# A three-layer attention stack on one core: order of projections, copies and loads around the starts of passes, and one semaphore count

## The chip, the cores and the metric

One core of a Trainium2 chip. The metric is the device time of one execution in microseconds (us), lower being better, given as the median of the runs shown. Engines: PE (TensorE), DVE (VectorE), ACT (ScalarE), POOL (GpSimd), SP (SyncE). A core is written by hand: each engine has its own list of instructions in program order, and semaphores tie the lists together.

## What is computed

One sequence of 1024 tokens of width 1024 goes through three layers, all in float32. Cut to what matters here:

```python
# layer 1: three mixers on the same projection
o_gla = gla_mixer(...)        # gated linear attention, 4 heads
o_dsa = dsa_mixer(...)        # top-256 keys by an indexer, then attention, 6 heads
y_pool = pool_mixer(...)      # windowed means
x = x + concat(y_gla, y_dsa, y_pool) @ w_out
# layer 2: "forgetting" attention, 16 heads, and a gated per-layer input
logit[t, s] = q_t . k_s / sqrt(d) + c[t] - c[s],  c = cumsum(log_sigmoid(h @ w_f + b_f))
h = h + (softmax(logit) @ v * silu(z)) @ w_out;  h = h + (p @ w_up) * sigmoid(h @ w_gate)
# layer 3: dilated attention, 8 heads, each the softmax over three patterns
DIL_PATTERN = ((128, 1), (512, 4), (2048, 16))       # window, stride
o = sum(softmax(stack(lses))[g] * attention_g(q_g, k_g, v_g))
h = h + (o * silu(z)) @ w_out;  h = h + (p @ w_up) * sigmoid(h @ w_gate)
```

## The kernel before

Activations lie transposed, features on the partitions and tokens in two halves of 512. A float32 product is made of three products of rounded parts: `products` (lines 887 to 889) multiplies high by high, high by low and low by high. One projection tile, `half_T`, is 8 such triples into one bank of PSUM, `proj[half]`; ACT copies it out (`projected`, line 1782). Counters join the two: PE waits on `pass_free[half]` before it fills the bank, ACT on `pass_done[half]` before it copies. A tile named X (`half_X`, line 916) turns the transposed values of a head around with 4 transposes through the same bank. Weights stream by SP into two slots and POOL splits them into high and low parts (lines 760 and 762).

The attention layers run in passes: 3 pairs of heads (`dsa`), 8 pairs (`fox`), 8 heads (`dil`). A pass has 8 steps of 128 query rows. While PE works through the steps of pass p, it also makes the projections of pass p+1, a few half tiles per step; `ORDER` names the tiles of a pass (for `dil` thirteen, `TTTTTTTTXTXTX`, so 26 halves), and `proj_units(kind, t)` gives the halves of step t in two parts. In the last pass no projections are left (`follow` is False).

A step of `dil` is this chain: PE makes the scores of a step in two pieces, each in its own bank (lines 1327 and 1336); DVE adds the distance bias piece by piece (line 2380, three adds a step) and takes the maximum (line 2390); ACT takes the exponential (line 1852); PE transposes the result (line 1357); ACT copies that (line 1862); PE multiplies with the values (lines 1380 and 1385); DVE scales (line 2403); PE turns the output (line 1346); DVE gates it (line 2424). `dil_sread` counts the second and the third add of each step, one for each piece. Before PE overwrites the scores of step s, piece b, it waits for `2s + b` of them:

```python
wait_pass(pe, S["sread"], p, N * pieces, s * pieces + piece)
```

On PE a pass of `dil` begins with the scores of steps 0 and 1, which wait until all 13 tiles are copied; on ACT it begins with the exponential of step 0, the store of the row of the head before (line 1788), and the tanh of the gate (line 1873).

The sparse attention (`dsa`) is started while DVE still sorts for the indexer: MAX8 and MATCH_REPLACE8 rounds (lines 2236 and 2238), between which DVE does other work at fixed rounds, among it `pool_outputs(1)`, which reads PE's `pool_products(1)` (line 1120). PE then makes the bias tables (line 1017) and the first scores (line 1182). ACT issues the loads of the bias rows (`load_bias`, line 1704) and the stores from its own queue. In its last pass PE also turns the reloaded input x tile by tile (`residual_turn`, line 1229), which SP loads (line 719) between the loads of finished rows (`finished_rows`, `late_row`, lines 675 and 681); `late_row` waits for the store of pass 1.

In the forgetting attention the rows of c go to memory (line 2020) and come back spread over the partitions (`decay`, line 1758), both issued by ACT.

## Time and profile before

| | us |
|---|---|
| runs, device time | 2986.93, 2995.12, 2994.61 (median 2994.61) |
| profiled execution, device time | 2991.6 |
| its span, first to last instruction | 2989.5 |
| PE matmul busy | 2841.3 (95%) |
| DVE, ACT, POOL busy | 1141.5, 900.4, 1022.8 |

The mean granted clock of TensorE in the profiled execution is 0.972 of full speed. Indexer and linear attention fill the first 480 us, the sparse attention runs to about 650 us, the forgetting attention from about 770 to 1410 us, the dilated attention from 1635 to 2790 us. A row of the timeline gives the start, the duration, the engine, the line and operation, `output<-input` by the program's names, the shape and the count of merged instructions; in brackets stands how long the engine was idle before and what released it. The profile counts some matmuls that the program writes once as two (32 in the profile for 16).

### The profile page before, as it was taken

The page shows a single profiled execution, that of the slowest core. Times are in us where ns is not written, and L with a number is a line of the kernel's source. Part 1 is how long each engine was busy: PE and PEld are TensorE (multiplying, and loading weights), DVE is VectorE, ACT ScalarE, POOL GpSimd, SP SyncE. Part 2 cuts the span into 40 slices and gives each one's busy share as a digit, 9 for nine tenths or more (in the row PEclk, how much of TensorE's full clock was granted, in tenths as well). Part 3 has the DMA queues.
Part 4 walks back from the last instruction along what each step waited for, and adds up shares of the span by engine and source line. Part 5 has one row for each costly group of instructions (what it writes and reads, how often), then busy time and mean ns, then how long its engine had stood idle before and what let it go on. Part 6 is the DMA issues. An engine that isn't in the chain of part 4 may idle for free.

```text
span 2989.5 us, 39787 instructions
## 1 busy us (share of the span) xinstructions
PE 2841.3 (95%) x16428; PEld 2208.0 (74%) x16428; DVE 1141.5 (38%) x2501; ACT 900.4 (30%) x1693; POOL 1022.8 (34%) x443
## 2 busy tenths in 40 slices
PE   6989998999899999999999999999999999998998
PEld 4756676667677777776887877778787878786886
DVE  7998995556422222224334011111111111114323
ACT  4322313552333333334113122222222222223112
POOL 2533392133222222223632433333333323333541
PEclk8989999999999999999999999999999999999998
DMA  4100121121211111112122111111111111113211
GB/s 100 41 22 22 29 67 58 57 78 37 65 39 35 48 50 50 50 43 92 57 78 64 43 43 36 43 42 44 43 43 36 43 43 43 42 44 127 71 44 62
DMA packets 222367, 155.02 MB, mean 52 GB/s; under 512 B 26294, under 2 KB 209116, under 8 KB 222060
## 3 DMA queue, kind: packets, MB, share of 16 engines
q1 hardware_dynamic: 210220, 122.62, 14.3%
q10 hardware_dynamic: 11968, 29.87, 2.7%
q8 instruction: 130, 2.13, 0.3%
q14 instruction: 49, 0.40, 0.0%
HBM read 132.99 MB, written 19.47 MB: 51 GB/s over the span
## 4 chain that ended last, share of the span: by engine, by line
PE 84%; DVE 7%; ACT 3%; issue 3%; POOL 2%; DMA 1%; ACTq 0%; DVEq 0%; SPq 0%; POOLq 0%
PE proj L887 21%; PE proj L889 20%; PE proj L888 20%; PE score L1182 3%; PE score L1197 3%; PE out L1212 3%; DVE arena L2236 1%; PE score L1327 1%; DVE arena L2238 1%; PE out L1380 1%; PE out L1385 1%; PE score L1357 1%; POOL w_lo L762 1%; POOL w_hi L760 1%; PE score L1336 1%
## 5 line engine op out<-in xcount | busy, mean ns | idle before, releaser
L887 PE MATMUL proj<-act_hi,w_hi 128*128 128x512 f32 x2560 | 1033.6, 404 | 21.4 <-ACT hT L1782 8.4
L888 PE MATMUL proj<-act_lo,w_hi 128*128 128x512 f32 x2560 | 1005.7, 393 | 0.0
L889 PE MATMUL proj<-act_hi,w_lo 128*128 128x512 f32 x2560 | 1005.5, 393 | 0.0
L760 POOL TENSOR_TENSOR w_hi<-w_raw,ones 128x1024 fp32r<-128x1024 f32 x177 | 425.4, 2404 | 1695.1 <-PE proj L889 1676.4
L887 PEld LDWEIGHTS proj<-act_hi,w_hi 128*128 128x128 f32 x2560 | 486.9, 190 | 135.0 <-issue 26.3
L889 PEld LDWEIGHTS proj<-act_hi,w_lo 128*128 128x128 f32 x2560 | 485.7, 190 | 105.0
L888 PEld LDWEIGHTS proj<-act_lo,w_hi 128*128 128x128 f32 x2560 | 487.2, 190 | 96.6 <-issue 0.2
L762 POOL TENSOR_TENSOR w_lo<-w_raw,w_hi 128x1024 fp32r<-128x1024 f32 x181 | 446.4, 2466 | 97.5 <-ACT w_hi L1936 83.6
L1782 ACT ACTIVATE arena<-proj 128x512 f32<-128x512 f32 x236 | 175.2, 752 | 691.5 <-PE proj L889 663.4
L2380 DVE SCALAR_TENSOR_TENSOR arena<-arena,score 128x256 f32<-128x256 f32 (+1 forms) x192 | 76.9, 428 | 770.9 <-PE score L1327 724.1
L2276 DVE CUSTOM_DVE_ANT_0 arena<-arena,score 128x512 f32<-128x512 f32 (+2 forms) x192 | 102.7, 572 | 371.1 <-PE score L1182 364.5
L1808 ACT ACTIVATE arena<-score 128x512 f32<-128x512 f32 (+3 forms) x264 | 116.0, 489 | 217.5 <-PE score L1197 217.3
L2236 DVE MAX8 arena<-arena 128x8 f32<-128x640 f32 (+5 forms) x176 | 162.6, 924 | 5.3
L2238 DVE MATCH_REPLACE8 arena<-arena 128x640 f32<-128x640 f32 (+5 forms) x176 | 159.8, 908 | 0.0
L1798 ACT ACTIVATE arena<-arena 128x256 f32<-128x256 f32 (+7 forms) x176 | 135.1, 773 | 68.5 <-DVE arena L2276 41.5
L1197 PEld LDWEIGHTS score<-ident,arena 128*128 128x128 f32 x792 | 87.1, 142 | 79.2 <-issue 48.8
L1782 ACT ACTIVATE hT<-proj 128x512 f32<-128x512 f32 x78 | 65.7, 849 | 260.7 <-PE proj L889 245.3
L1197 PE MATMUL score<-ident,arena 128*128 128x128 f32 x792 | 119.8, 285 | 7.2 <-ACT arena L1798 6.7
L1182 PE MATMUL score<-arena 64*128 64x512 f32 (+3 forms) x432 | 101.5, 547 | 0.7 <-DVE arena L2288 0.7
L887 PE MATMUL proj<-res_parts,w_hi 128*128 128x512 f32 x256 | 101.5, 397 | 0.0
L889 PE MATMUL proj<-res_parts,w_lo 128*128 128x512 f32 x256 | 101.4, 396 | 0.0
L888 PE MATMUL proj<-res_parts,w_hi 128*128 128x512 f32 x256 | 101.4, 396 | 0.0
(260 smaller groups left out, 2881.3 us busy)
## 6 DMA issues: line engine op xcount, KB each, us to landing
w_raw<-dil_w_in_dram SPq DMA_DIRECT2D x80, 512.0 KB, 3.7
w_raw<-fox_w_in_dram SPq DMA_DIRECT2D x32, 512.0 KB, 4.1
w_raw<-w_in_dram SPq DMA_DIRECT2D x23, 512.0 KB, 3.8
y_scratch<-arena ACTq DMA_DIRECT2D x21, 512.0 KB, 4.7
act_lo<-y_scratch SPq DMA_DIRECT2D x21, 512.0 KB, 6.0
arena<-decay_scratch ACTq DMA_DIRECT2D x16, 512.0 KB, 6.8
w_raw<-ple_w_gate_dram SPq DMA_DIRECT2D x16, 512.0 KB, 3.9
arena<-x_dram SPq DMA_DIRECT2D x12, 512.0 KB, 4.0
```

The source lines that it names most:

```text
L760: pool.tensor_tensor(hi, raw, one.unsqueeze(1).broadcast_to([P, KB, P]), ALU.mult).then_inc(w_hi_done, 1)
L762: pool.tensor_tensor(lo, raw, hi.bitcast(F32), ALU.subtract).then_inc(w_split, 1)
L887: pe.matmul(bank, hi, a_hi, start=first, stop=False)
L888: pe.matmul(bank, hi, a_lo, start=False, stop=False)
L889: return pe.matmul(bank, lo, a_hi, start=False, stop=last)
L1182: mm = pe.matmul(score[:, 0, hh * 512:hh * 512 + w], Q["q"][0][rows, i * P:(i + 1) * P], Q["k"][0][rows, lo:lo + w], start=not masked, sto ...
L1197: mm = pe.transpose(score[:, 1, hh * 512 + b * P:hh * 512 + (b + 1) * P], R["p"][hh][i % 2][:, (b0 + b) * P:(b0 + b + 1) * P], ident[:, :])
L1782: act.activation(dst, src, ACT.Copy, scale=scale if role == "q" else 1.0).then_inc(pass_free[half], 1)
L1798: act.activation(R["p"][hh][i % 2][:, 0:width], R["p"][hh][i % 2][:, 0:width], ACT.Exp, bias=R["st"][:, s:s + 1], scale=-1.0, accum_out=R[ ...
L1808: act.activation(R["pT"][hh][:, q % 2, 0:nb * P], score[:, 1, hh * 512:hh * 512 + nb * P], ACT.Copy).then_inc(S["te"], 1)
L2236: dve.max(top8, scores[:, 0:w]).then_inc(IX["top"], 1)
L2238: dve.match_replace(row, top8, row, -3e38).then_inc(IX["top"], 1)
```

## The change

It has five parts.

1. Dilated scores wait for `2(s-1) + b + 1` adds: those of the same piece in the step before.
2. `proj_units` leaves out the last tile of a pass (X, both halves), holds at most two halves in the first part, and puts the second half of an X tile and what follows it into a third part, the tail. For `dil` that changes steps 5 and 6: step 5 was X8.0, X8.1, T9.0, scores of step 7, values; it is X8.0, scores, X8.1, T9.0, values. Step 6 was T9.1, X10.0, X10.1, values; it is T9.1, X10.0, values, X10.1 (the number is the place in `ORDER`, the digit behind the point the half). The last tile X12 is made at the start of the pass that uses it: half 0 behind the scores of step 0, half 1 behind those of step 1. PE waits for one tile fewer at the start, and for the last one before the values of step 0. ACT copies X12 behind the exponential and the store, ahead of the tanh.
3. At the start of the sparse attention two of the four half tiles of pass 2 made ahead (`PAIR_HALVES[2:4]`) move behind `pool_products(1)` and the bias tables, one behind each of the first two score steps; ACT copies them behind the first exponential. `load_bias` is issued one copy sooner.
4. `late_row("dsa")` moves on SP from ahead of the reload of x tile 2 to ahead of that of tile 4.
5. `decay(0, 0)` of the forgetting attention moves on ACT behind two copies of projections.

```diff
@@ proj_units @@
-    units = [(h // 2, h % 2, None) for h in range(first, last)]
-    early = 2 if kind == "dil" else 1
-    return units[:early], units[early:]
+    units = [(h // 2, h % 2, None) for h in range(first, last) if h // 2 < len(ORDER[kind]) - 1]
+    ready = [u for u in units if ORDER[kind][u[0]] != "X" or u[1] == 0]
+    n = next((i for i, u in enumerate(units) if u not in ready), len(units))
+    early = min(n, 2)
+    return units[:early], units[early:n], units[n:]
@@ SP @@
-                    sp.wait_ge(pass_done[half], base + PASSES[kind] * len(ORDER[kind]))
+                    sp.wait_ge(pass_done[half], base + PASSES[kind] * len(ORDER[kind]) - (1 if kind == "dil" else 0))
                         finished_rows("dsa", C_DSA)
+                    if t == 4:
                         late_row("dsa")
@@ PE, sparse attention @@
                     scores(0, 0)
+                    if kind == "dsa" and p == 0:
+                        project(2, [(b, half, None) for b, half in PAIR_HALVES[2:3]])
                     scores(1, 0)
+                    if kind == "dsa" and p == 0:
+                        project(2, [(b, half, None) for b, half in PAIR_HALVES[3:4]])
...
-                    project(2, halves[0:4])
+                    project(2, halves[0:2])
                     pool_products(1)
@@ PE, dilated attention @@
-                        wait_pass(pe, S["sread"], p, N * pieces, s * pieces + piece)
+                        wait_pass(pe, S["sread"], p, N * pieces, (s - 1) * pieces + piece + 1)
...
-                        pe.wait_ge(pass_free[half], p * NB + first + NB)
+                        pe.wait_ge(pass_free[half], p * NB + first + NB - (1 if p > 0 else 0))
                     for piece in range(pieces):
                         scores(0, piece)
                     if p > 0:
+                        project(p, [(NB - 1, 0, None)])
                         turn(N - 2, p - 1)
                         turn(N - 1, p - 1)
                     scores(1, 0)
+                    if p > 0:
+                        project(p, [(NB - 1, 1, None)])
...
                         if t + 2 < N:
                             scores(t + 2, 0)
+                        if follow and t + 2 < N:
+                            project(p + 1, tail)
+                        if t == 0 and p > 0:
+                            for half in range(2):
+                                pe.wait_ge(pass_free[half], p * NB + first + NB)
                         for c in range(0 if len(chunks[t]) <= 2 else 2, 4):
                             values(t, c)
+                        if follow and t + 2 >= N:
+                            project(p + 1, tail)
@@ ACT @@
+                    if kind == "dsa" and p == 0:
+                        projected(2, 2, [(b, half, None) for b, half in PAIR_HALVES[2:4]])
...
-                        act.wait_ge(pass_free[half], p * NB + (base + NB))
+                        act.wait_ge(pass_free[half], p * NB + (base + NB) - (1 if p > 0 else 0))
...
+                    if p > 0:
+                        projected(p, turn_, [(NB - 1, half, None) for half in range(2)])
                     act.activation(R["e"], Q["g"], ACT.Tanh, scale=0.5).then_inc(S["gate"], 1)
...
-                decay(0, 0)
...
-                    projected(1, 1, halves[4:6])
+                    projected(1, 1, halves[4:5])
                     load_bias()
-                    projected(1, 1, halves[6:])
+                    projected(1, 1, halves[5:])
...
+                    if kind == "fox":
+                        projected(0, 0, halves[2:4])
+                        decay(0, 0)
+                    projected(0, 0, halves[4:])
```

The order of PE around the start of a dilated pass, before, from the last matmul of the last tile (L916 is a tile of kind X, L1380 and L1385 the values of step 7, L1327 and L1336 the two pieces of the scores, L1346 the turns of the outputs, L1357 the transposes of step 0):

```order
L889 MATMUL proj<-act_hi,w_lo 128x512
L916 MATMUL proj<-ident,arena 128x128 x8
L1380 MATMUL out<-arena 32x128 x16
L1385 MATMUL out<-arena 128x128 x2
L1327 MATMUL score<-hT 32x128 x8
L1336 MATMUL score<-hT 128x128
L1346 MATMUL out<-ident,arena 128x128 x2
L1327 MATMUL score<-hT 32x128 x8
L1357 MATMUL score<-ident,arena 128x128 x3
L1336 MATMUL score<-hT 128x256
L887 MATMUL proj<-act_hi,w_hi 128x512
```

And in the changed kernel, whose lines there are numbered 3 or 7 higher:

```order
L892 MATMUL proj<-act_hi,w_lo 128x512
L1387 MATMUL out<-arena 32x128 x16
L1392 MATMUL out<-arena 128x128 x2
L1334 MATMUL score<-hT 32x128 x8
L1343 MATMUL score<-hT 128x128
L919 MATMUL proj<-ident,arena 128x128 x4
L1353 MATMUL out<-ident,arena 128x128 x2
L1334 MATMUL score<-hT 32x128 x8
L919 MATMUL proj<-ident,arena 128x128 x4
L1364 MATMUL score<-ident,arena 128x128 x3
L1343 MATMUL score<-hT 128x256
L890 MATMUL proj<-act_hi,w_hi 128x512
```

The eight transposes of X12 left the place ahead of the values and stand in two fours between scores, turns and transposes.

ACT at the same place, before and in the changed kernel (the 128x512 copies are of projections, the 128x384 row is the exponential of step 0, the 128x1024 ones the store and the tanh):

```order
L1782 ACTIVATE arena<-proj0 128x512
L1782 ACTIVATE arena<-proj1 128x512
L1782 ACTIVATE arena<-proj0 128x512
L1782 ACTIVATE arena<-proj1 128x512
L1852 ACTIVATE arena<-arena 128x384
L1788 DMA y_scratch<-arena 128x1024
L1873 ACTIVATE arena<-arena 128x1024
```

```order
L1801 ACTIVATE arena<-proj0 128x512
L1801 ACTIVATE arena<-proj1 128x512
L1873 ACTIVATE arena<-arena 128x384
L1807 DMA y_scratch<-arena 128x1024
L1801 ACTIVATE arena<-proj0 128x512
L1801 ACTIVATE arena<-proj1 128x512
L1896 ACTIVATE arena<-arena 128x1024
```

The two copies of X12 moved from ahead of the exponential to behind it.

## Rows read from the trace of the kernel before

**Rows 1.** The page's table of busy time: engine, us, share of the span, instructions

```profile
PE 2841.3 (95%) x16428; PEld 2208.0 (74%) x16428; DVE 1141.5 (38%) x2501; ACT 900.4 (30%) x1693; POOL 1022.8 (34%) x443
```

**Rows 2.** PE's longest group of waits in 2003:2145, one dilated pass: us, times, longest

```profile
PE proj L916 <- ACT arena L1782: 1.0, 2, 0.7
```

**Rows 3.** Timeline of PE at one start of a pass: start, us, what, [idle before]

```profile
2010.23 0.60 PE L916 MATMUL proj<-ident,arena 128*128 128x128 f32 x4
...
2011.66 1.08 PE L1380 MATMUL out<-arena 128*32 128x128 f32 x32
...
2013.32 0.64 PE L1327 MATMUL score<-hT 128*32 128x128 f32 x16
2014.76 0.49 PE L1336 MATMUL score<-hT 128*128 128x128 f32 x2 [0.80 <-DVE arena L2380]
...
2017.02 0.55 PE L1357 MATMUL score<-ident,arena 128*128 128x128 f32 x3 [0.68 <-ACT arena L1852]
...
2017.64 0.58 PE L887 MATMUL proj<-act_hi,w_hi 128*128 128x512 f32 x1
```

**Rows 4.** Timeline of DVE and of ACT in the same stretch

```profile
2015.29 0.35 DVE L2380 SCALAR_TENSOR_TENSOR arena<-arena,score 128x128 f32<-128x128 f32 x1 [0.58 <-PE score L1336]
...
2016.26 0.62 ACT L1852 ACTIVATE arena<-arena 128x384 f32<-128x384 f32 x1 [3.89 <-DVE arena L2390]
...
2017.08 1.06 ACT L1873 ACTIVATE arena<-arena 128x1024 f32<-128x1024 f32 x1
```

**Rows 5.** Timeline of PE in steps 5 and 6 of a pass

```profile
2120.06 1.04 PE L916 MATMUL proj<-ident,arena 128*128 128x128 f32 x8
2121.44 0.47 PE L887 MATMUL proj<-act_hi,w_hi 128*128 128x512 f32 x1 [0.34 <-POOL w_lo L762]
...
2136.14 0.60 PE L916 MATMUL proj<-ident,arena 128*128 128x128 f32 x4
...
2138.04 0.64 PE L1380 MATMUL out<-arena 128*32 128x128 f32 x16
```

**Rows 6.** Stretches: us, busy of PE, PEld, DVE, ACT, POOL, then granted clock, DMA

```profile
441.00:445.00 4.00, 3.80 (x10) 3.05 (x11) 3.90 (x5) 0.06 (x1) 3.92 (x3) 0.57 0.35 100
488.00:496.00 8.00, 6.76 (x24) 4.04 (x25) 6.38 (x29) 4.74 (x16) 0.00 (x0) 0.51 0.40 140
1874.00:1879.00 5.00, 4.67 (x15) 3.78 (x16) 2.74 (x5) 1.71 (x4) 0.00 (x0) 0.66 0.63 208
```

**Rows 7.** Last dilated pass: PE's longest group of waits; one DVE row

```profile
PE score L1327 <- DVE arena L2380: 7.6, 7, 2.8
...
2732.38 1.94 DVE L2428 TENSOR_TENSOR act_lo<-arena,act_hi 128x128 fp32r<-128x128 f32 x1
```

**Rows 8.** Timelines of ACT and PE where the sparse attention begins

```profile
437.67 2.74 ACTq L1704 DMA_DIRECT2D arena<-bias_scratch  x6
...
441.20 0.75 PE L887 MATMUL proj<-act_hi,w_hi 128*128 128x512 f32 x1 [3.14 <-ACT hT L1782]
...
477.08 1.88 PE L1120 MATMUL out<-arena 128*128 128x512 f32 x4
...
488.56 1.22 PE L1182 MATMUL score<-hT 64*128 64x256 f32 x4 [3.91 <-DVE arena L2288]
```

**Rows 9.** Timelines of PE and DVE in the last sparse pass

```profile
603.81 1.97 PE L1229 MATMUL proj<-ident,arena 128*128 128x128 f32 x8 [4.00 <-DMA arena<-x_dram]
...
608.86 1.09 PE L1197 MATMUL score<-ident,arena 128*128 128x128 f32 x8
...
602.58 2.56 DVE L2296 CUSTOM_DVE_ANT_0 arena<-arena 128x256 f32<-128x256 f32 x1
```

**Rows 10.** Timelines of PE and ACT before the forgetting attention

```profile
784.45 0.47 PE L887 MATMUL proj<-act_hi,w_hi 128*128 128x512 f32 x1 [3.42 <-ACT arena L1782]
...
780.92 0.31 ACTq L2020 DMA_DIRECT2D decay_scratch<-arena  x1
...
783.70 1.09 ACT L1782 ACTIVATE arena<-proj 128x512 f32<-128x512 f32 x2 [7.56 <-DMA decay_scratch<-arena]
```

11 lines of the change are left out of this document (6 added, 5 removed).

## The prediction

> **What bounds the kernel now.** I read the page first: PE is busy for 2841.3 of 2989.5 us [rows 1], so nearly all the time is PE's own work and a change of order can give back only idle time of PE, some 148 us, and time at the lower clock. The table of granted clock and busy time by stretch shows where that lies: the middle of the program has little, the two ends and the starts of passes have more. Then the list of PE's waits, stretch by stretch, says who releases it; in the dilated layer it is the same list in every pass, and it begins with tiles of kind X that wait for a bank [rows 2]. The timelines of PE, DVE and ACT at those places [rows 3 to 5, 7 to 10] give the order of the waits. The reader should look there at two things: the bracket, which is a wait, and the distance between two starts, which also holds what the bracket leaves out.
>
> **The start of a dilated pass (7 times).** From X12 to the next pass's first tile PE needs 7.41 us, 2010.23 to 2017.64 [rows 3]. What holds it is a chain: scores, three adds, maximum, exponential, transposes. Two things shorten it. X12 stands ahead of the values now and delays the chain by 1.43 us (2011.66 - 2010.23); in the new order it lies in the chain's idle places, since PE waits 0.80 and 0.68 us there and more around the turns. And the second piece of the scores no longer waits for the adds of the first, so that DVE loses its 0.58 us ahead of the third add [rows 4]. That is 2.0 us. Against it stands the new place of the copies of X12: behind the exponential. ACT is free 0.82 us after the exponential starts (2017.08 - 2016.26, rows 4), a copy takes 0.6, so the bank is free at 1.42 us; PE wanted it at 1.38 us (2017.64 - 2016.26). With the semaphore I take 0.15 us for that. Net 1.85 us, times 7: **13.0**. Bounds: 1.3 (only the moved X12, less the hold) and 2.2 each. The tanh comes 1.2 us later; its reader, the gate on DVE, and the copy of the transposes have 16 us of projections as cover, except in the last pass. If that cover went, it would cost those 1.2 us a pass.
>
> **Steps 5 and 6 (7 passes each).** Eight transposes in a row take 0.9 us of PE (1.04 with the end of the last). In step 5 tile T9.0 starts 1.38 us after X8 [rows 5]: the row blames POOL, but the bank freed by the copy of X8.0 falls at the same time, and the weights were asked for long before. With scores and X8.1 between, that copy is covered: 0.5 us. ACT now copies X8.1 behind the exponential of step 6; a whole half tile of projection stands between it and its user. In step 6 the eight transposes of X10 take 1.90 us up to the values (2138.04 - 2136.14), because X10.1 waits 0.7 us for a copy; behind the values it doesn't wait: 1.0 us. Together 7 x 1.5 = **10.5**, bounds 6 and 11.
>
> **First and last dilated pass.** In the first there is no X12 to move, only the 0.58 us: **0.6**. In the last there are no projections, so the chain is bare. Seven waits of scores for adds take 7.6 us [rows 7]; they were waits for the later piece, and the count per piece removes them. What is late next is the exponential: the chain from one step's second scores through adds, maximum and exponential is then the period. I followed it step by step through the timeline and got 4.5 us back in eight steps, after the later tanh, which is no longer covered here. Half of it is the one wait of 2.8 us behind a DVE subtraction that took 1.94 us instead of the 0.29 of its undisturbed kind. **4.5**, bounds 0 and 8.
>
> Here a rule speaks against the change. The row shows the 1.94 us subtraction [rows 7] ending as POOL's own subtraction ends, and others with 2.2 us. The Trainium skill, page "SBUF — State Buffer", section "SBUF: two separate sides", says that DVE and GpSimd share a port pair held for a whole instruction, so that the loser blocks fully. By that rule the chain stays as long as POOL's instructions decide, and each step can meet the lock anew; the sum would have 0 here in place of 4.5. The trace agrees with the lock. I keep 4.5, since three of the steps had no lock and still waited.
>
> **Clock.** After the start of a pass the clock is at 1.2 instead of 2.4 GHz for a while: in 1874 to 1879 the grant is 0.66, which costs 5 x 0.34 = 1.7 us [rows 6]. Four such stretches lie in the dilated layer, 6 to 7 us in all, each behind a start of a pass or behind the 2.8 us wait; the other starts have the same waits and full clock. With most of the idle time gone I expect half back: **3**, bounds -4 and 6.5.
>
> The Trainium skill, page "TensorE: Matmul & The Clock Gate", section "A second HAM failure mode: psum-queue depth-cycling", says that micro-idles between groups of matmuls suffice to make the clock swing. By that rule all of the 6.5 us would come back, 3.5 more than my sum. The trace bears it out only in part, since the same idle pattern gave a low clock at some starts and not at others.
>
> **Start of the sparse attention.** ACT spends 2.74 us issuing the bias loads while a copy waits behind them, and PE stands still for 3.14 us [rows 8]. One copy sooner the issue falls into 4.8 us in which ACT has nothing; the usual wait at such a place, 0.7 us, is left. 2.4 us, and the low clock behind it, 4 x 0.43 = 1.7 [rows 6]. Then DVE: its last three sort rounds can't begin before PE has made `pool_products(1)` at 477.08, and 11.5 us later, at 488.56, PE still waits 3.91 us for it. Two half tiles, 10.9 us of projection, move from ahead of line 1120 to behind it, so the wait is filled, and of the low clock in 488 to 496 (6.76 x 0.49 = 3.3) some 2.3. New: the tanh is behind the copy of the second moved half, so the first values wait for 0.6 + 1.06 us and an ordinary copy, 1.2 us more than now. 3.9 + 2.3 - 1.2 = 5.0. Together **9.1**, bounds 5 and 12.
>
> **Reload of x.** PE waits 4.00 us for tile 2 [rows 9], whose load stood on SP's queue behind `late_row`, and so behind ACT's store. With that moved two tiles on, the load is issued when the tile 0 buffer is free, 5 us sooner. What ends the wait next is DVE: its 2.56 us operation of step 3 ends at 605.14, the exponential and transposes follow at about 606.0 and not at 608.86. **2.8**, bounds 0.8 and 4. The late row is needed two steps after its new place.
>
> **Decay rows.** ACT holds two copies behind a wait of 7.56 us for the store of the decay rows; PE stands still for 3.42 us [rows 10]. Ahead of that wait, the copies start when the store is issued, at 781.23 instead of 783.70: **2.5**, bounds 2 and 3.4. The load of the rows moves by nothing that counts, 30 us ahead of its use.
>
> **Sum.** 13.0 + 10.5 + 0.6 + 4.5 + 3 + 9.1 + 2.8 + 2.5 = 46.0 us off the profiled execution's 2991.6: 2945.6. The median of the runs shown is 3.0 above that execution, so 2948.6, given as 2949. A difference of 0.3% or 9 us is about what a measurement can tell from no change.
>
> **Rivals.** (a) The clock takes part of it: the idle time left (0.65 us at a pass start, 1.8 us in the sparse attention) still brings the low clock, and at seven starts instead of three. That is 3 + 4 x 1.7 + 2.3, some 12 us less, and with the last pass giving 0, 16.5: 2965. For it: the lower clock follows waits of very different lengths. Against: 3.4 us of waiting before 784.45 brought none. (b) The order does nothing where I count most: if the X tiles' waits only move to the next copy, steps 5, 6 and the starts give 3 instead of 23.5, and the rest stands: 2969. For it: PE and ACT share one bank per half. Against: the copies that T11 and T9 need are then older by a whole group of values. (c) Slower: ACT becomes the holder. X8.1 and X12 now stand behind an exponential that waits for DVE, and X12 also behind the store, 14 places in all. If such a hold lasted as long as the one ACT has at the decay rows, 7.56 us, at each place, it would cost 106 us: 2949 + 106 = 3055. It decides from (46 + 9) / 14 = 3.9 us a place. Against: the maximum that releases the exponential is done within 1 us of its adds, as rows 4 show for the exponential of step 0. (d) The new count frees nothing, because in passes with projections the wait is long met; this holds already for six of eight steps and is in the sum, so it isn't a case of its own.
>
> **How the numbers follow.** The forecast has 0.72, (a) 0.13, (b) 0.08, (c) 0.03; 0.04 for anything that brings it within 9 us of before. The time is the forecast's, 2949. The bounds of the terms don't all fall together: added with weight on the low side they give 2937 to 2962, and (a) and most of (b) reach to 2968. Range 2936 to 2969. Faster by over 0.3%: 0.72 + 0.13 + 0.08 = 0.93; within: 0.04; slower: 0.03.
>
> **What would show it.** A dilated pass should take 138.7 us in place of 142. In PE's waits there the groups at L916 (1.0 us) and at L1336 (0.8) should be gone, and the one before the transposes of step 0 be left with about 0.65. DVE's three adds of step 0 should follow without a gap. Near 440 and 488 the waits of 3.14 and 3.91 us should be gone, and one of about 1.8 stand before the first values. The wait at L1229 should be gone. It is wrong if new waits of PE for ACT's copies stand before the first tile of a pass, or if the mean granted clock, 0.972 before, falls.

## The result, and the profile after

| | before | changed |
|---|---|---|
| device time, median of 4 runs, us | 2994.86 (2986.93 to 2996.82) | 2945.47 (2939.50 to 2949.02) |
| ratio | | 0.9841, 95% interval 0.9819 to 0.9863 |
| profiled execution: device time, span | 2991.6, 2989.5 | 2939.5, 2937.4 |
| mean granted clock of TensorE | 0.972 | 0.980 |

The changed kernel is 49.4 us faster by the medians; predicted were 46 us, to 2949. Run again later beside a new set of runs of the kernel before it had a ratio of 0.9826 (0.9809 to 0.9843). The profiled executions are 52.1 us apart, and this is what the landmarks below add up to.

The changed kernel's page, table of busy time, against [rows 1]. PE has 20.8 us less, with the same instructions: that is time at the full clock instead of the lower one, since a matmul takes longer at 1.2 GHz. By the mean clocks some 84 us of clock were missing before (0.028 x 2989.5) and 59 after (0.020 x 2937.4).

```profile
PE 2820.5 (96%) x16428; PEld 2192.5 (75%) x16428; DVE 1135.5 (39%) x2501; ACT 899.6 (31%) x1693; POOL 1023.9 (35%) x443
```

**Dilated pass.** A pass without low clock takes 138.04 us from tanh to tanh; it took 141.06. Against [rows 2] stands the whole list of PE's waits in one pass (us, times, longest):

```profile
PE score L1364 <- ACT arena L1873: 0.2, 1, 0.2
```

The start of that pass, against [rows 3]: timeline of PE.

```profile
1985.50 1.08 PE L1387 MATMUL out<-arena 128*32 128x128 f32 x32
...
1988.06 0.60 PE L919 MATMUL proj<-ident,arena 128*128 128x128 f32 x4
...
1989.38 0.66 PE L919 MATMUL proj<-ident,arena 128*128 128x128 f32 x4
1990.19 0.55 PE L1364 MATMUL score<-ident,arena 128*128 128x128 f32 x3 [0.15 <-ACT arena L1873]
...
1991.02 0.47 PE L890 MATMUL proj<-act_hi,w_hi 128*128 128x512 f32 x1
```

From the values (L1387) to the next pass's first tile (L890) it is 5.52 us; before, the same way was 5.98 us, 2011.66 to 2017.64, with the 1.43 us of X12 ahead of it. That is 0.46 + 1.43 = 1.89 us; X12 lies in two places that were idle. DVE and ACT there, against [rows 4]: the adds of step 0 are now one group of three without a gap, and X12's copies stand between the exponential and the tanh.

```profile
1987.94 0.87 DVE L2405 SCALAR_TENSOR_TENSOR arena<-arena,score 128x128 f32<-128x128 f32 x3 [0.26 <-PE score L1334]
```

```profile
1989.43 0.62 ACT L1873 ACTIVATE arena<-arena 128x384 f32<-128x384 f32 x1 [3.22 <-DVE arena L2415]
...
1990.28 1.09 ACT L1801 ACTIVATE arena<-proj 128x512 f32<-128x512 f32 x2
1991.25 1.06 ACT L1896 ACTIVATE arena<-arena 128x1024 f32<-128x1024 f32 x1
```

Steps 5 and 6, against [rows 5]. From X8 to T9.0 PE is at work all the time, scores included; in step 6 the values start 0.53 us after X10.0 (2109.68 - 2109.15) and not 1.90 us, and X10.1 comes behind them.

```profile
2093.32 0.60 PE L919 MATMUL proj<-ident,arena 128*128 128x128 f32 x4
2093.85 1.07 PE L1334 MATMUL score<-hT 128*32 128x256 f32 x16
2094.85 0.66 PE L919 MATMUL proj<-ident,arena 128*128 128x128 f32 x4
2095.26 0.48 PE L890 MATMUL proj<-act_hi,w_hi 128*128 128x512 f32 x1
...
2109.15 0.60 PE L919 MATMUL proj<-ident,arena 128*128 128x128 f32 x4
2109.68 0.64 PE L1387 MATMUL out<-arena 128*32 128x128 f32 x16
...
2111.24 0.60 PE L919 MATMUL proj<-ident,arena 128*128 128x128 f32 x4
```

**Last dilated pass**, PE's waits in 2683:2714, against [rows 7]. The group of 7.6 us is gone. The first values wait 1.1 us (the tanh is ahead of the copy that they need). From the exponential of one step to that of the next, steps 3 to 4, 5 to 6 and 6 to 7 took 5.75, 5.96 and 5.97 us and now take 3.50, 3.93 and 3.93; steps 2 to 3 take 5.5 us in both kernels.

```profile
PE out L1353 <- DVE arena L2428: 1.2, 2, 1.0
PE out L1387 <- issue: 1.1, 1, 1.1
PE out L1387 <- DVE arena L2449: 0.7, 1, 0.7
```

The kernel before had two stretches at the lower clock here, the changed one has none. The first begins at 2735.0 and lies between the exponentials; the second begins at 2758.9, behind the last of them at 2757.07. The kernel before, columns as in [rows 6]:

```profile
2734.00:2739.00 5.00, 4.24 (x42) 3.13 (x43) 3.00 (x9) 1.76 (x3) 4.24 (x3) 0.66 1.05 440
2758.00:2763.00 5.00, 4.84 (x18) 3.95 (x19) 1.19 (x6) 1.80 (x5) 2.37 (x1) 0.66 0.00 0
```

**Start of the sparse attention**, PE, against [rows 8]. The wait of 3.14 us is 0.83, `pool_products(1)` comes 16.8 us sooner (1.95 of them are from the opening, whose code is unchanged), and the wait of 3.91 us does not occur. New is the 1.75 us ahead of the first values, and the clock falls behind it: the matmul at 483.78 takes 0.77 us instead of the 0.47 of the one at 436.94.

```profile
436.94 0.47 PE L890 MATMUL proj<-act_hi,w_hi 128*128 128x512 f32 x1 [0.83 <-ACT hT L1801]
...
460.26 1.02 PE L1123 MATMUL out<-arena 128*128 128x512 f32 x2
...
481.81 0.44 PE L1215 MATMUL out<-arena,hT 128*64 128x128 f32 x4 [1.75 <-ACT arena L1827]
...
483.78 0.77 PE L890 MATMUL proj<-act_hi,w_hi 128*128 128x512 f32 x1
```

**Reload of x and decay rows**, PE, against [rows 9, 10]: 4.00 us have become 1.55, and 3.42 us have become 1.01.

```profile
589.10 1.09 PE L1232 MATMUL proj<-ident,arena 128*128 128x128 f32 x8 [1.55 <-DMA arena<-x_dram]
...
764.17 0.47 PE L890 MATMUL proj<-act_hi,w_hi 128*128 128x512 f32 x1 [1.01 <-ACT arena L1801]
```

**Where the 52.1 us come from**, by the distance between landmarks in the two profiled executions:

| from, to | before | changed | gain |
|---|---|---|---|
| start, `pool_products(0)` (code unchanged) | 424.85 | 422.90 | 1.95 |
| to the third tanh of the sparse attention | 166.90 | 156.64 | 10.26 |
| to the last turn of x | 38.55 | 35.63 | 2.92 |
| to the first tanh of the forgetting attention | 182.41 | 177.26 | 5.15 |
| to its last tanh (code unchanged) | 546.33 | 546.19 | 0.14 |
| to the first tanh of the dilated attention | 372.63 | 374.00 | -1.37 |
| to its last tanh | 992.35 | 968.83 | 23.52 |
| to the end | 260.60 | 251.05 | 9.55 |

The last landmark lies 4.9 us ahead of the end of the span in both.

### The profile page after: what moved, and what is told of

Its sections match the earlier page's. It is cut to its first block, busy times and chain, and to the rows that moved or that the text cites. A ratio compares the mean times of both kernels' runs of the same rounds, so it can differ in the third digit from the quotient of the medians.

```text
span 2937.4 us, 39794 instructions
## 1 busy us (share of the span) xinstructions
PE 2820.5 (96%) x16428; PEld 2192.5 (75%) x16428; DVE 1135.5 (39%) x2501; ACT 899.6 (31%) x1693; POOL 1023.9 (35%) x443
## 3 DMA queue, kind: packets, MB, share of 16 engines
q8 instruction: 130, 2.13, 0.3%
## 4 chain that ended last, share of the span: by engine, by line
PE 86%; DVE 7%; ACT 3%; issue 3%; DMA 1%; POOL 1%; ACTq 0%; DVEq 0%; POOLq 0%
PE proj L890 21%; PE proj L892 21%; PE proj L891 21%; PE score L1185 3%; PE score L1200 3%; PE out L1215 3%; PE score L1334 1%; PE out L1387 1%; DVE arena L2261 1%; PE score L1364 1%; PE out L1392 1%; DVE arena L2263 1%; DMA y_scratch<-arena 1%; PE proj L919 1%; PE score L1343 1%
## 5 line engine op out<-in xcount | busy, mean ns | idle before, releaser
L890 PE MATMUL proj<-act_hi,w_hi 128*128 128x512 f32 x2560 | 1030.0, 402 | 14.3 <-ACT hT L1801 6.1
L890 PEld LDWEIGHTS proj<-act_hi,w_hi 128*128 128x128 f32 x2560 | 485.2, 190 | 126.9 <-issue 21.2
L1801 ACT ACTIVATE arena<-proj 128x512 f32<-128x512 f32 x236 | 175.8, 753 | 682.5 <-PE proj L892 657.3
L890 PE MATMUL proj<-res_parts,w_hi 128*128 128x512 f32 x256 | 101.5, 397 | 0.0
```

What stands on the lines that cost most here:

```text
L890: pe.matmul(bank, hi, a_hi, start=first, stop=False)
L1801: act.activation(dst, src, ACT.Copy, scale=scale if role == "q" else 1.0).then_inc(pass_free[half], 1)
```

## The experiments

All times of a stretch are from the profiled execution of the kernel named, counted between the same landmarks. Edits are shown against the changed kernel unless said otherwise, in the direction in which they were made.

**1. The count alone undone.**

```diff
-wait_pass(pe, S["sread"], p, N * pieces, (s - 1) * pieces + piece + 1)
+wait_pass(pe, S["sread"], p, N * pieces, s * pieces + piece)
```

> The changed kernel with the old count alone: the second piece of the scores waits again for the adds of the first. Theory (my step: 0.58 us per pass start, and the waits of the last pass): a dilated pass takes 138.0 + 0.6 = 138.6 us, the last one 3 to 5 us more; in all some +8 us against the changed kernel. Rival 1 (X12 between the scores covers the count too): the pass stays at 138.0, only the last one is longer. Rival 2 (the count is what keeps the clock up): passes with the low clock come back at 1.7 us each, mean above 139.

Measured: ratio to the kernel before 0.9893 (0.9870 to 0.9916), median 2959.36 us. A pass takes 139.00 us, 0.97 more and not 0.6. In the last pass, from the first exponential of step 0 to the last exponential, 33.9 us instead of 27.5: the waits of [rows 7] are back, and with them the two stretches at the lower clock, one of them behind the last exponential. Together that is 7 x 0.97 + 6.4 = 13.2 us, where +8 were expected.

PE's waits in one pass and, behind the dots, in the last one, 2684:2720:

```profile
PE score L1343 <- DVE arena L2405: 0.8, 1, 0.8
...
PE score L1334 <- DVE arena L2405: 7.4, 6, 2.8
```

It follows that in the new order the count is worth 6.4 us in the last pass, the clock included, and almost 1 us per start. Rival 1 falls; rival 2 too for the passes with projections, none of which has a low clock that the changed kernel has not.

**2. X12 back in its old place.**

```diff
 proj_units:
-    units = [... for h in range(first, last) if h // 2 < len(ORDER[kind]) - 1]
+    units = [... for h in range(first, last)]
 PE, start of a pass:
-                        project(p, [(NB - 1, 0, None)])
...
-                        project(p, [(NB - 1, 1, None)])
 ACT, start of a pass:
-                        projected(p, turn_, [(NB - 1, half, None) for half in range(2)])
```

Not shown: the waits of PE and ACT that count the last tile go back too, and the halves of X12 stay out of the tail.

> The changed kernel with X12 back ahead of the values of the last step; the halves of X8 and X10 and the count stay changed. Theory (1.43 us of chain less 0.15 of hold): a dilated pass takes 138.0 + 1.3 = 139.3 us, the tanh of a pass comes 1.2 us sooner after the exponential, the last pass loses 1.2 us at its start; in all +8 us. Rival 1 (the hold behind the exponential eats the move): pass 138.0 to 138.4. Rival 2 (the chain costs all of 1.43 and the tanh's delay nothing in the last pass): 139.4 and +10 us.

Measured: ratio 0.9872 (0.9853 to 0.9891), median 2952.48. A pass takes 139.33 us, 1.29 more: 1.43 of the chain less 0.15 of the hold, as the theory has it. In the last pass the way from the first exponential to the last is 26.2 us against 27.5 us. Only 0.4 us of this is the later tanh: in experiments 4 and 9, which have the tanh early and the rest of this pass as in the changed kernel, the way is 27.1 and 27.0 us. The other 0.8 to 0.9 us come from a subtraction of DVE that starts just ahead of one of POOL here and inside it there; the last section has more on it.

**3. The second halves of X8 and X10 back.**

```diff
 proj_units:
+    n = len(units)
     early = min(n, 2)
```

> The changed kernel with the second halves of X8 and X10 back ahead of scores and values; X12 and the count stay changed. Theory (0.5 us in step 5, 1.0 in step 6): a dilated pass takes 138.0 + 1.5 = 139.5 us, waits of PE at the X tiles' line and at the line of the transposes of step 6 (1.0 and 0.8 us before) come back; in all +10.5 us. Rival (the waits only moved to the next copy, rival b of the prediction): pass 138.0 to 138.3 us, within 2 us in all.

Measured: ratio 0.9873 (0.9854 to 0.9892), median 2953.51. A pass takes 139.14 us: 1.10 more, not 1.5. PE's waits in one pass have 0.7 us at the X tiles again, and POOL's 0.3:

```profile
PE proj L920 <- ACT arena L1802: 0.7, 1, 0.7
PE proj L891 <- POOL w_lo L766: 0.3, 1, 0.3
```

The rival (waits only move) falls. Laid beside the changed kernel from tanh to tanh, step 5 is 0.32 us longer (7.89 against 7.57 from X8 to the values) and step 6 is 0.81 us longer (4.14 against 3.33 from X10 to the next projection).

**4. The count alone, in the kernel before.** The edit of experiment 1 the other way round, nothing else.

> The kernel before with the new count alone. Undone alone in the changed kernel it cost 0.97 us per dilated pass, and the three parts undone one by one cost 3.37 us per pass together, against 3.02 between the two kernels, so some of them cover for one another. Theory (only DVE's gap of 0.58 us lies in the old chain): a pass takes 141.06 - 0.6 = 140.5 us, the last pass is 4 to 7 us shorter, -9 us in all. Rival 1 (the count's worth does not depend on the order): 140.1 us. Rival 2 (it frees nothing while X12 stands ahead of the values): 141.0 us, and only the last pass is shorter.

Measured: ratio 0.9950 (0.9936 to 0.9965), median 2975.71, 15 us less where 9 were expected. A pass takes 140.40 us, 0.66 less; the last pass is 6.8 us shorter between its exponentials. One low stretch lies in those 6.8 us and is gone too. So the count's worth per pass depends on the order, 0.66 us in the old one and 0.97 in the new. The three parts undone one by one cost 0.97 + 1.29 + 1.10 = 3.36 us, and together they give 3.02: 0.34 us is counted twice. The way to the first dilated tanh is 371.99 us instead of 372.63, 0.64 us for the first pass.

This execution has no stretch at the lower clock in the dilated layer, where the kernel before has five, although each pass with projections still has 1.0 us of waits at the X tiles and 1.9 us ahead of transposes (line 1357). So the clock did not need the new order of the tiles to come back.

**5. The ends undone, dilated layer as changed.** The four edits outside the dilated layer taken back.

> The changed kernel with the dilated layer as changed and the rest undone: two half tiles ahead of the pool's exponentials, bias loads, late row and decay rows at their old places. Theory: +13 us, of which 8 at the start of the sparse attention (waits of 3.1 and 3.9 us back), 2.9 at the reload of x (4.0 us wait), 2.4 at the decay rows; dilated pass unchanged at 138.0. Rival (part of what these landmarks show is the clock's own luck from run to run): the two waits come back and the landmarks differ by less than 10 us.

Measured: ratio 0.9900 (0.9884 to 0.9916), median 2961.09. Dilated pass 138.04 us, the same. From `pool_products(0)` to the third tanh 166.74 us, where the kernel before has 166.90 and the changed one 156.64; to the last turn of x 37.79 us, and from there to the tanh of the forgetting attention 179.50. That is 10.1, 2.2 and 2.2 us more than in the changed kernel, where 8, 2.9 and 2.4 were expected. The waits of 3.9 and 3.1 us are back, and the rival (less than 10 us in all) falls.

**6. The half tiles alone, 7. the bias loads alone.**

```diff
 experiment 6, PE and ACT:
-                    project(2, halves[0:2])
+                    project(2, halves[0:4])
...
-                    projected(2, 2, halves[0:2])
+                    projected(2, 2, halves[0:4])
 experiment 7, ACT:
-                    projected(1, 1, halves[4:5])
+                    projected(1, 1, halves[4:6])
                     load_bias()
-                    projected(1, 1, halves[5:])
+                    projected(1, 1, halves[6:])
```

Not shown: in experiment 6 the two half tiles behind the first score steps and their copies behind the first exponential are taken out.

> The changed kernel with the two half tiles of projection back ahead of the pool's exponentials and their copies back ahead of the tanh. Theory (3.9 of wait, 2.3 of clock, less 1.2): the wait of 3.9 us for DVE's adds near 485 is back, the first values wait about 0.7 instead of 1.75 us, and the first tanh of the sparse attention comes 5 us later than in the changed kernel's runs, counted from pool_products(0). Two runs with the old order had 51.4 us from the second to the third tanh against 49.0 in four with the new one: if the half tiles decide this, it is 51.4 here. Rival (the bias loads decide it): 49.0 here.

> The changed kernel with the bias loads issued one copy later, as before. Theory (2.4 of wait, 1.7 of clock): PE waits 3.1 us near 438 for a copy, a stretch at the lower clock follows it, and the first tanh of the sparse attention is 4.1 us later than in the changed kernel's runs, counted from pool_products(0); 49.0 us from the second to the third tanh. Rival 1 (DVE's sort is the bound of this stage, so the wait only fills the later one): 0 to 1 us. Rival 2 (the bias loads decide the stretch of low clock in the second pass): 51.4 us between the second and third tanh.

Measured (one run each): to the first tanh 60.84 us without the moved half tiles and 61.33 us with the late bias loads, against 57.47 with both moves and 64.8 with neither. The two are 3.4 and 3.9 us, together 7.2 of 7.3: they do not cover for one another, and rival 1 of experiment 7 falls. The first tanh itself stands behind two more copies in the new order, which hides part of what the half tiles are worth; the second tanh has the same place in all of them. Up to there it is 111.73 and 111.45 us, against 107.60 with both moves and 115.50 with neither: the half tiles are worth 4.1 us, not the expected 5, and the bias loads 3.9 us, together 7.9. PE's waits in 430:500, first of experiment 6, then of 7:

```profile
PE score L1185 <- DVE arena L2307: 3.9, 1, 3.9
PE proj L890 <- ACT hT L1797: 1.6, 2, 0.8
PE out L1215 <- ACT arena L1823: 1.1, 2, 0.7
```

```profile
PE proj L890 <- ACT hT L1801: 3.9, 2, 3.1
PE out L1215 <- ACT arena L1827: 2.2, 2, 1.7
```

From the second to the third tanh both have over 51 us (51.54 and 51.64), not 49.0. So neither of the two parts decides this step of 2.4 us; more on it under experiment 9.

**8. The late row and the decay rows undone.**

```diff
 SP:
-                    if t == 4:
-                        late_row("dsa")
+                        late_row("dsa")
 ACT, before the forgetting attention:
+                decay(0, 0)
...
-                        projected(0, 0, halves[2:4])
-                        decay(0, 0)
```

> The changed kernel with the late row and the decay rows at their old places. Theory: PE waits 4.0 us for the third tile of x again, and the last turn of x comes 2.3 to 2.9 us later after the third tanh (38.2 against 35.8); PE waits 3.4 us before the forget attention again, and its first tanh is 2.1 us later, the low clock of the stretch taken off (175.8 against 173.7). Rival (the reload's wait belonged to the old order ahead of it): one of the two segments stays as in the changed kernel.

Measured (one run): 38.33 us from the third tanh to the last turn of x, 2.7 more than the changed kernel; the next stretch, up to the forgetting attention's tanh, 183.91 us less some 8.6 at the lower clock, 175.3, against 173.9. PE's waits at the two places:

```profile
PE proj L1231 <- DMA arena<-x_dram: 4.4, 1, 4.4
...
PE proj L889 <- ACT arena L1800: 5.0, 3, 3.4
```

Both terms hold, the second at the lower end: it is 1.4 us by this pair, and 2.0 us by the other three executions with the old place (175.6, 176.1, 175.8) against the ten with the new one (173.5 to 174.0). Low clock is taken off here, and below, as the missing share of the grant in windows of 2 us. That supposes that PE sets the pace in the whole stretch.

**9. Three more moves on ACT.** The waits that the changed kernel has left: in the first sparse pass the tanh goes between the two copies of half tiles, in each dilated pass the copy of X12's first half goes ahead of the exponential, and in the last one the tanh goes behind the copy of the transposes.

```diff
 ACT, sparse attention, first pass:
-                        projected(2, 2, [(b, half, None) for b, half in PAIR_HALVES[2:4]])
+                        projected(2, 2, [(b, half, None) for b, half in PAIR_HALVES[2:3]])
...
                     act.activation(R["e"], Q["g"], ACT.Tanh, scale=0.5).then_inc(S["gate"], 1)
+                    if kind == "dsa" and p == 0:
+                        projected(2, 2, [(b, half, None) for b, half in PAIR_HALVES[3:4]])
 ACT, dilated pass:
+                    if p > 0:
+                        projected(p, turn_, [(NB - 1, 0, None)])
                     exp(0)
...
+                    if follow:
                         act.activation(R["e"], Q["g"], ACT.Tanh, scale=0.5).then_inc(S["gate"], 1)
...
+                        if not follow and t == 0:
+                            act.activation(R["e"], Q["g"], ACT.Tanh, scale=0.5).then_inc(S["gate"], 1)
```

> The changed kernel with three more moves on ACT: in the first sparse pass the tanh between the two copies (so that the first values no longer wait 1.75 us for it), in every dilated pass the copy of the first half of X12 ahead of the exponential, and in the last dilated pass the tanh behind the copy of the transposes of step 0 (its values waited 1.14 us). Theory: first values wait about 0.7 us and the 1.7 us of low clock behind that wait are gone, 1 to 2.7 us; the last pass 0.8 us; a dilated pass 0.2 to 0.4 us shorter (137.7), as the transposes and the next pass's first tile no longer wait for ACT; 4 to 6 us in all. Rival 1 (the copy ahead of the exponential delays it, since X12's first half comes only 0.8 us before it): pass 138.2 to 138.6, in all slower than the changed kernel. Rival 2 (ACT's holds are covered): pass 138.0.

Measured: ratio 0.9844 (0.9825 to 0.9863), median 2944.98: no difference to the changed kernel. All three moves did locally what they were meant to. The first values of the sparse attention wait 0.81 us (1.75 before the move), and no low clock follows. But the second pass, 47 us on, now starts at the lower clock: its transposes of X take 1.06 us, not 0.60. The third tanh comes 156.31 us after `pool_products(0)`, against 156.64: the second tanh was still 2.5 us ahead, and 0.3 of the hoped for 1 to 2.7 us is left at the third.

```profile
481.79 0.44 PE L1215 MATMUL out<-arena,hT 128*64 128x128 f32 x4 [0.81 <-ACT arena L1827]
...
528.91 1.06 PE L919 MATMUL proj<-ident,arena 128*128 128x128 f32 x4
```

A dilated pass takes 137.95 us instead of 138.04: rival 2, the hold was covered but for 0.1 us. In the last pass the wait of 1.1 us fell to 0.3, and the last exponential came 163.66 us after the tanh of the pass before, against 163.72. That tanh is itself 0.5 us earlier against its exponential now, though; from the first exponential of the last pass to the last it is 27.04 us against 27.47, so 0.4 of the 0.8 us is left, as much as there is at the exponential of step 2 already. DVE's rows of step 3, 2684:2690, show what the chain meets next. DVE waits for the store of the last head row, and then its subtraction meets one of POOL.

```profile
2686.79 0.29 DVE L2454 SCALAR_TENSOR_TENSOR act_hi<-out,arena 128x128 fp32r<-128x128 f32 x1 [1.10 <-DMA y_scratch<-arena]
...
2687.39 1.73 DVE L2460 TENSOR_TENSOR act_lo<-arena,act_hi 128x128 fp32r<-128x128 f32 x1
```

**10. The store ahead of the loads.** SP issues 3 MB of finished rows just before ACT's store; four of the six loads now wait for it.

```diff
 SP, finished_rows:
                 for j, k in enumerate(rows_before(m)[:6]):
+                    if kind == "dil" and j == 2:
+                        sp.wait_ge(AT[kind]["ysent"], 16 * (STORES_BEFORE[kind] + PASSES[kind] - 1))
```

> The changed kernel, but in the dilated layer SP issues four of the six loads of finished rows behind the store of the last head row (a wait on that store). Theory: DVE's wait of 2.13 us in the last pass for the store (9.2 us to landing beside 3 MB of loads, where 4.0 is the median) is what holds the chain there, so the store lands in about 4 us, the wait is gone, and the last values come 1.5 to 2.1 us sooner than 163.3 us after the tanh of the pass before. Rival 1 (the wait lies beside another chain, or POOL's lock takes its place, as it did when the tanh was moved): within 0.3 us. Rival 2 (the held loads come late for ACT's splits): ACT waits for DMA in the last pass and the values come later than 163.3.

Measured: ratio 0.9835 (0.9815 to 0.9854), median 2945.04, the changed kernel beside it (experiment 11) 2941.82. The store lands 2.6 us after its issue, DVE's wait for it, 2.13 us in the changed kernel, is gone and the exponential of step 3 comes 2.28 us sooner (146.15 against 148.43 us after the tanh of the pass before). The last one comes 0.90 us sooner (162.82 against 163.72), where 1.5 to 2.1 were expected. Between them the subtraction of the next step met POOL's: first the changed kernel, then this one.

```profile
2689.38 0.29 DVE L2447 SCALAR_TENSOR_TENSOR act_hi<-out,arena 128x128 fp32r<-128x128 f32 x1 [2.13 <-DMA y_scratch<-arena]
...
2693.52 0.29 DVE L2453 TENSOR_TENSOR act_lo<-arena,act_hi 128x128 fp32r<-128x128 f32 x1
```

```profile
2694.16 0.28 DVE L2449 SCALAR_TENSOR_TENSOR act_hi<-out,arena 128x128 fp32r<-128x128 f32 x1
...
2698.57 1.43 DVE L2455 TENSOR_TENSOR act_lo<-arena,act_hi 128x128 fp32r<-128x128 f32 x1
...
2695.14 7.08 POOL L772 TENSOR_TENSOR act_lo<-act_lo,act_hi 128x1024 fp32r<-128x1024 f32 x3 [7.47 <-ACT act_hi L1761]
```

POOL's row is three subtractions of 2.36 us; the second ends at 2699.86, and DVE's 1.43 us end at 2700.00.

The wait is gone as the theory says, and 1.14 of the 2.3 us go to the lock, as rival 1 has it. It was not the length of the wait that held the chain, though: 2694.74, where the subtraction of step 3 starts now, is 0.4 us ahead of POOL's start, and in the changed kernel it started behind that and ended with POOL's.

**11. The changed kernel again**, on the chip and beside the runs of experiments 8, 10 and 12.

> The changed kernel once more, to stand beside the next ones. Both theories: ratio 0.984; a dilated pass of 138.04 us; what differs between two executions should be whole steps of 1.7 us of low clock, and not the waits.

Measured: 2941.82 us (2939.93 to 2943.40), ratio 0.9826 (0.9809 to 0.9843). Every interval between tanhs of the dilated layer is within 0.05 us of the first profile's.

**12. All four extra moves together**, with the tanh of the first sparse pass behind the first copies of transposes.

> All of it together: the store first, in the last pass the tanh behind the copy of the transposes of step 0, the copy of X12's first half ahead of the exponential, and in the first sparse pass the tanh behind the first copies of transposes instead of between the two projection copies. Theory: the wait at the first values of the sparse attention is 0.8 instead of 1.75 us; whether its second pass starts at low clock can't be said, it has 49.0 or 51.4 us to the third tanh; last values about 161 us after the tanh of the pass before; a pass 137.95 us; 2 to 5 us less than the changed kernel. Rival (the clock gives it back, as it did when the tanh alone was moved): the same time as the changed kernel, with a low stretch at the start of the second sparse pass.

Measured: 2940.98 us (2939.28 to 2944.71), ratio 0.9825 (0.9808 to 0.9843), against 2941.82 of the changed kernel on the same chip: the same. From the first exponential of the last pass to the last it is 26.17 us against 27.47: the 0.4 us of experiment 9 and the 0.9 us of experiment 10 add. A pass takes 137.96 us; the second sparse pass again starts at the lower clock. None of the versions tried beats the changed kernel by what can be measured.

## Why the prediction was right

The forecast was 46.0 us; its terms measure 48.4 us. They are taken from the experiments where one isolates them, and otherwise from the landmarks. The mechanisms hold, and the sum comes closer than its terms: steps 5 and 6 were put 2.8 us too high and the clock of the dilated layer 3.8 us too low, and 2.4 us at the start of the sparse attention were not foreseen.

| term of the sum | predicted | measured | from |
|---|---|---|---|
| starts of 7 passes | 13.0 | 13.4 | 7 x (3.02 - 1.10) |
| steps 5 and 6, 7 passes | 10.5 | 7.7 | experiment 3, 7 x 1.10 |
| first pass | 0.6 | 0.6 | experiment 4 |
| last pass | 4.5 | 4.7 | 33.87 - 27.47 between exponentials, less 1.7 of clock |
| clock in the dilated layer | 3 | 6.8 | low stretches in 1700 to 2765 |
| start of the sparse attention | 9.1 | 10.3 | landmarks |
| reload of x | 2.8 | 2.9 | landmarks; 2.7 in experiment 8 |
| decay rows | 2.5 | 2.0 | experiment 8 |

The other 3.7 us of the 52.1 lie in unchanged code: 1.95 in the opening, 3.1 before and -2.0 behind the forgetting attention, 0.5 in the output stage, 0.1 elsewhere. They go with the clock: against the kernel before, low stretches are 1.7 us of clock shorter in the opening, 3.4 shorter before and 1.7 longer behind the forgetting attention. So the clock has a far larger part in the difference than the 3 + 1.7 + 2.3 = 7 us of the forecast: by the mean clocks 25 us of it came back over the whole program, not all of them where PE sets the pace.

**Starts of passes.** A pass takes 138.04 us and not 138.7: the 142 of the forecast is near the mean of seven passes, low clock included, and a pass without it took 141.06. The term is right as to mechanism and size, and the two largest figures of its working stand: 1.43 less 0.15 of hold (1.29 measured), and 0.58 for DVE's gap (0.66 in the old order). The tanh comes 1.0 us later against the exponential in the seven passes that have an X12 to copy, and is covered in the six of them that have projections. The hold that was to be "about 0.65" ahead of the transposes is 0.15 us.

**Steps 5 and 6** were mis-sized: 0.32 us instead of 0.5, and 0.81 instead of 1.0. The step that failed is "eight transposes in a row take 0.9 us": the X tile is no longer in a row. Its halves apart cost 0.53 + 0.41 = 0.94 us in step 5 (the rows at 2093.32 and 2094.85 up to the next) and 0.53 + 0.43 = 0.96 in step 6, and what lies between them becomes longer too: the scores between X8.0 and X8.1 take 1.00 us where they take 0.88 in experiment 3, and the turn and transposes behind X10.1 take 0.81 us where they take 0.68 there.

**Last pass.** The count is its whole gain: 6.8 us put alone into the kernel before, less 0.4 for the later tanh. Of the 6.4 us between the two kernels one low stretch is clock, 1.7 us taken whole, and 4.7 are left; the other stretch lies behind the last exponential. What such a stretch costs here is less than that: the executions of experiments 3 and 7, whose last pass is that of the changed kernel, have one and need 28.4 us instead of 27.5, 0.9 us. By that price 5.5 are left. The 4.5 had half of it at the one wait of 2.8 us; steps 3 to 4 are 2.25 us shorter, and 5 to 6 and 6 to 7 2.0 us each. The rule of the Trainium skill, page "SBUF — State Buffer", section "SBUF: two separate sides", by which the sum would have had 0, describes what happens (1.43 to 1.94 us instead of 0.29), and at one step it decides: steps 2 to 3 gained nothing (5.48 and 5.50 us). But the chain as a whole did not stay as long as POOL decides: in the changed kernel the later subtractions, as the one at 2693.52, run free. In experiment 10 the lock took back 1.1 us of the 2.3 that a shorter wait had given. It is right per instruction and too strong as a forecast of a stage.

**Clock.** This is the term that was furthest off, 3 against 6.8, above its own upper bound of 6.5. Five low stretches of 1.7 us lay in the dilated layer, at 1731, 1874, 2158, 2735 and 2758, not four, and they became one at 1712. The step that failed is "I expect half back". The rule of the Trainium skill, page "TensorE: Matmul & The Clock Gate", section "A second HAM failure mode: psum-queue depth-cycling", would have given 6.5 us, and by the number it was the better forecast here. That the small waits had to go for it isn't shown: in experiment 4 all five are gone with most of the waits still in place. The last section shows a stretch where equal waits had either clock.

**Start of the sparse attention.** The waits of 3.14 and 3.91 us went and the new one before the first values is 1.75 us, 1.8 forecast. The two moves were worth 4.1 and 3.9 us up to the second tanh, 5.0 and 4.1 forecast, and they add: 7.9 for the 9.1. That 10.3 were measured is luck. What the sum did not have is a step of 2.4 us in the second pass, whose start no longer falls to the lower clock.

**Reload, decay rows.** 2.9 and 2.0 us, 2.8 and 2.5 forecast. The wait at L1229 was said to go; 1.55 us of it stayed, and it is the load that ends it. The gain came out right since DVE's 2.57 us operation behind it sets the same end. In the executions of experiments 1 and 6 PE waits less than 0.4 us for the tile, and the way to the last turn of x is the same 35.8 and 35.7 us.

**Rivals.** (a) fell: the mean clock rose from 0.972 to 0.980. (b) fell by experiment 3. (c) fell: ACT holds no copy that PE waits for by more than 0.2 us in a pass, against the 3.9 us a place at which it would have decided. (d) is true for the steps and not for the start and the last pass, where the count gives 0.66 us and 6.8 us, a low stretch included.

## What to carry to other kernels

Where a semaphore counts reads of several banks, write down for each wait the read that frees that bank; one count too many cost 0.66 us in covered passes and 6.8 us (0.9 to 1.7 of it at the lower clock) in the one pass without cover, and the edit is one line. Work that is cut in two to fill idle places cost some 0.2 us at each of the two cuts measured (0.5 against 0.32 and 1.0 against 0.81). And once PE is 96% busy, moving one wait further is worth trying in whole stages only: three moves that each removed the wait they aimed at (0.9, 0.8 and 2.1 us) gave nothing that can be measured in sum. In the profile 1.3 of the 2.9 us of the last two are left, 1.1 went to a lock, and the 2.0 to 2.5 us that the first had given up to the second tanh were lost to the clock before the third. A landmark that the edit itself moves, as the tanh was here, hides such a gain or makes one up.

## What the runs showed of the hardware

**The clock does not follow from the rows just ahead.** Experiment 10 does not differ from the changed kernel in anything before the dilated layer. In the second execution of the changed kernel and in that of experiment 10 the start of the second sparse pass has the same rows with the same idle times; then one goes on at full clock and the other at half. PE, first the changed kernel (experiment 11), then experiment 10:

```profile
530.86 0.71 PE L1200 MATMUL score<-ident,arena 128*128 128x128 f32 x2 [0.62 <-ACT arena L1817]
531.41 0.60 PE L919 MATMUL proj<-ident,arena 128*128 128x128 f32 x4
532.93 0.44 PE L1215 MATMUL out<-arena,hT 128*64 128x128 f32 x4 [0.92 <-ACT arena L1827]
533.30 0.92 PE L1185 MATMUL score<-hT 64*128 64x384 f32 x4
```

```profile
530.76 0.71 PE L1202 MATMUL score<-ident,arena 128*128 128x128 f32 x2 [0.62 <-ACT arena L1819]
531.31 0.60 PE L921 MATMUL proj<-ident,arena 128*128 128x128 f32 x4
532.83 0.70 PE L1217 MATMUL out<-arena,hT 128*64 128x128 f32 x4 [0.92 <-ACT arena L1829]
533.46 1.65 PE L1187 MATMUL score<-hT 64*128 64x384 f32 x4
```

The same stretch of ten microseconds in both (us, busy times, then the granted clock), 1.00 and 0.66:

```profile
530.00:540.00 10.00, 8.40 (x52) 5.33 (x52) 7.13 (x32) 5.73 (x19) 0.12 (x1) 1.00 0.14 55
```

```profile
530.00:540.00 10.00, 8.40 (x34) 5.64 (x32) 6.63 (x29) 5.81 (x18) 0.02 (x1) 0.66 0.14 55
```

That costs 2.7 us (51.66 against 48.99 from the second tanh to the third). Of seven profiled executions with the new code up to there one had it; of seven in which the start of the sparse attention was ordered otherwise (the kernel before, experiments 4 to 7, 9 and 12) all seven had it. So the order of the work some 50 us earlier goes with how often it happens, and doesn't settle it. What it is that carries over was not isolated. The first sparse pass shows the same with the wait of 1.75 us: of the seven executions with that code six go to the lower clock right behind it, and that of experiment 1 does not (48.51 us from the first tanh to the second, 50.1 in the others).

**A store behind loads.** The store of a head row, 512 KB, usually lands 4.0 us after its issue by the page; beside 3 MB of loads that SP issued 4 us sooner it took 9.2 us, and DVE waited for it. Two thirds of the loads held back, it landed after 2.6 us and that wait was gone.

**What a low stretch costs.** Where 1.7 us of clock were missing in one stretch, the second and the fourth dilated pass of the kernel before took 142.41 and 142.70 us from tanh to tanh, not 141.06, so 1.4 and 1.6 us more. In the last pass, where PE stands idle for part of the time, it was 0.9 us (experiments 3 and 7).

**DVE and POOL.** The subtraction of 128x128 took 0.29 us at most steps and 1.43, 1.73 and 1.94 us at others, with the same operands; a move of 1 us in the chain decides which steps are met. At step 3 of the last pass DVE first waits for the store. In 11 of the 14 profiled executions this wait had lengths from 0.76 to 2.15 us, and wait and subtraction together were 2.81 to 2.84 us in every one of them: the subtraction ended 0.15 us behind POOL's first, whenever it had started. In the other three (experiments 2, 10 and 12) the wait was at most 0.20 us, the subtraction started 0.1 to 0.4 us ahead of POOL's and took 0.29 us. So up to a point shortening such a wait gives nothing, and then some 2 us at once.
